# Scores, routing and dot products from an input that is not divided by its rms; head 0's query by columns as they come; w_ada tiles and gather slots reordered

## What is computed

```python
x = x + gate1 * (y_mix @ w_out)
h2 = rms_norm(x, norm2_w) * (1.0 + scale2) + shift2      # scale2, shift2 from silu(c) @ w_ada + b_ada
q = (h2 @ peer_wq)                                       # 8 heads, 2 halves of 128
s = q . peer_subkeys                                     # 2 x 128 scores a head
vals, idx = top_k(s, 16); combo = sum of pairs           # 16 x 16
top_s, pos = top_k(combo, 16); expert = ids[pos]
g = softmax(top_s); a = gelu(peer_u[expert] . h2)
x = x + gate2 * sum((g * a) * peer_v[expert])
```

## Time and profile before

| | |
|---|---|
| median of 3 runs | 1179.93 us (1179.10 to 1180.93) |
| the profiled execution, its own time | 1180.36 us |
| its span (first to last instruction) | 1178.4 us |
| PE / PEld / DVE / ACT / POOL busy | 89% / 83% / 71% / 37% / 23% |
| gathers (queue 0) | 268.45 MB, 55.0% of 16 engines' span |
| weight loads (queue 1) | 120.10 MB, 27.8% |

### The profile page before, as it was taken

How to read it: one execution, slowest core, us unless ns; L and a number is a source line. 1 busy time by engine, 2 the same in 40 slices (tenths; PEclk the granted TensorE clock), 3 DMA queues, 4 the chain that set the end, 5 groups by cost and what they waited for, 6 DMA issues and landing times.

```text
span 1178.4 us, 18884 instructions
## 1 busy us (share of the span) xinstructions
PE 1051.1 (89%) x7587; PEld 980.2 (83%) x7587; DVE 837.5 (71%) x1801; ACT 433.0 (37%) x913; POOL 268.8 (23%) x289
## 2 busy tenths in 40 slices
PE   8999987999999987777877778878999999999997
PEld 6999986998899877777877777778899888898886
DVE  7978889667667667666776766655756868765776
ACT  3635832123212221222122122211557654476452
POOL 1000005343334333333333333434000000300000
PEclk9999999999999999998999999989999999999999
DMA  9965988999999999999999999999854655455540
GB/s 371 406 244 180 348 313 307 420 421 420 421 420 420 421 420 421 420 421 420 420 420 421 420 421 422 420 422 420 325 208 161 237 205 184 147 211 179 186 171 36
DMA packets 59480, 390.35 MB, mean 331 GB/s; under 512 B 6785, under 2 KB 7809, under 8 KB 15618
## 3 DMA queue, kind: packets, MB, share of 16 engines
q0 software_dynamic: 36864, 268.45, 55.0%
q1 hardware_dynamic: 21056, 120.10, 27.8%
q10 hardware_dynamic: 1474, 0.60, 0.2%
HBM read 388.08 MB, written 1.05 MB: 330 GB/s over the span
## 4 chain that ended last, share of the span: by engine, by line
PE 63%; DMA 24%; DVE 6%; ACT 4%; issue 1%; SPq 0%; another core or an unknown queue 0%; DVEq 0%; ACTq 0%
DMA rows<-in_peer_uv,work 23%; PE aux L1566 23%; PE pj L1609 6%; PE pj L1611 5%; PE pj L1610 5%; PE aux L1545 5%; PE pj L1286 5%; PE pj L1287 4%; PE pj L1288 4%; DVE rows L2061 2%; DMA rows<-in_w_ada 1%; PE aux L1360 1%; ACT work L1142 1%; ACT rows L1010 1%; PE aux L1425 1%
## 5 line engine op out<-in xcount | busy, mean ns | idle before, releaser
L1566 PE MATMUL aux<-work,rows 128*128 128x128 f32 x2080 | 263.4, 291 | 73.8 <-ACT work L1142 73.8
L1566 PEld LDWEIGHTS aux<-work,rows 128*128 128x128 f32 x2080 | 256.2, 206 | 81.6 <-ACT work L1142 81.4
L1566 PE MATMUL aux<-work,low_pairs 128*128 128x128 f32 x2016 | 238.2, 279 | 30.2 <-ACT work L1142 30.1
L1566 PEld LDWEIGHTS aux<-work,low_pairs 128*128 128x128 f32 x2016 | 233.0, 195 | 34.0 <-ACT work L1142 34.0
L898 POOL DMA_INDIRECT rows<-in_peer_uv,work x130 | 125.5, 965 | 301.2 <-PE aux L1566 232.1
L707 DVE TENSOR_TENSOR wlo<-wring,whi 128x1024 fp32r<-128x1024 f32 x100 | 121.0, 1235 | 77.6 <-ACT whi L701 77.1
L898 POOL DMA_INDIRECT low_pairs<-in_peer_uv,work x126 | 118.3, 939 | 158.5 <-PE aux L1566 153.4
L1286 PE MATMUL pj<-xh,whi 128*128 128x256 f32 x512 | 146.3, 286 | 0.4
L1137 ACT ACTIVATE work<-work 128x4 f32<-128x4 f32 (+2 forms) x71 | 14.7, 207 | 358.3 <-DVE work L2061 358.3
L1287 PE MATMUL pj<-xl,whi 128*128 128x256 f32 x512 | 144.8, 283 | 0.0
L1288 PE MATMUL pj<-xh,wlo 128*128 128x256 f32 x512 | 144.8, 283 | 0.0
(11 more groups left out here) (288 smaller groups left out, 1461.5 us busy)
## 6 DMA issues: line engine op xcount, KB each, us to landing
wring<-in_w SPq DMA_DIRECT2D x76, 1024.0 KB, 4.8
rows<-in_w_ada SPq DMA_DIRECT2D x40, 512.0 KB, 10.1
low_pairs<-in_w_ada SPq DMA_DIRECT2D x1, 4096.0 KB, 13.4
rows<-in_w SPq DMA_DIRECT2D x3, 1024.0 KB, 10.4
rows<-in_peer_uv,work POOLq DMA_INDIRECT x130
work<-in_late_rows SPq DMA_DIRECT2D x2, 1024.0 KB, 7.5
xT<-in_gate_rows SPq DMA_DIRECT2D x2, 1024.0 KB, 7.2
rows<-in_norm_rows SPq DMA_DIRECT2D x2, 1024.0 KB, 7.3
```

What stands on the lines that cost most here:

```text
L1566: ins = mm(peer_sum[t][:, c * P:(c + 1) * P], pair(n)[:, D + c * P:D + (c + 1) * P], diag[:, n % PICKS, :], start=(n % (EXPERT_HEADS * PIC ...
```

## The change

1. **Undivided input.** `hT` becomes x * gain + r * shift, that is h2 * r. The queries, scores and dot products are then r times their values; r is positive, so the picks stay. The factor 1 / r (`token_inv`) enters as the `scale` of the softmax's exponential and of the gelu; PE turns the root to token-major (`turn_rms`), VectorE inverts two columns of it in `route(0)`.
2. **Who makes it.** ScalarE multiplies by the gain (`times_gain`, between the squares) and makes r * shift (`shift_rows`, over `work`); POOL adds the two for tile 0 (one 128x1024 addition ahead of the gathers), VectorE for tile 1 (behind `route(0)`).
3. **Head 0's query.** PE multiplies x * gain for columns 0 to 5, then 6 and 7, as they come (`early_products`, 16 products); the shift's part is a product of the weights with the shift vector alone (16 products with one column, behind `sum_v` of tile 1 and ahead of `turn_y`), and VectorE joins them: r * that + the product.
4. **Head 1** of tile 0 is also scored early (`early_query_of_head_1`), and `score_query` / `score_keys` of head 1 do tile 1 only.
5. **w_ada.** 46 tiles through the ring, two behind the projection (1 MB in place of 4 MB, slot 8). The added six are loaded behind units 12 to 14; five dot products lie between the splits of pieces 11 and 12. The shift's and gain's columns are ready before the projection.
6. **Slots.** In all rounds but the last, pick n % 12 goes to slot `FIRST_ORDER[n % 12]`; a pick waits for the last pick that had its slot.
7. `keep_busy` makes 8 fillers where it made 4; gate exponentials of groups 0 and 1 move in ScalarE's order.

```diff
-OWN_GROUPS = ((OWN_UNIT, ), (HELD_QUERY, *SUB_UNITS), FIRST_HEADS)
+OWN_GROUPS = ((OWN_UNIT, ), (HELD_QUERY, *SUB_UNITS), FIRST_HEADS[:1], FIRST_HEADS[1:])
-ADA_AFTER = {4: range(16, 21), 7: (21, 22), 8: (23, 24), 9: (25, ), 13: range(26, 29), 18: range(29, 34), 22: (34, ), 20: (35, ), 25: (36, 37), 27: (38, 39)}
+ADA_AFTER = {4: range(16, 21), 7: (21, 22), 8: (23, 24), 9: (25, ), 12: range(26, 31), 13: range(31, 34), 14: (34, 35), 18: range(36, 41), 22: (41, ), 20: (42, ),
+             25: (43, 44), 27: (45, )}
-LOWS_AMONG_PICKS = (6, 7, 7, 8, 8, 9, 10, 11)
+LOWS_AMONG_PICKS = (6, 7, 7, 8, 9, 10, 10, 11)
+FIRST_ORDER = (0, 1, 6, 7, 9, 10, 11, 2, 3, 4, 8, 5)
+LAST_ROUND = LAST_PICK // SLOTS * SLOTS - SLOTS
+def slot(n):
+    return n % SLOTS if n >= LAST_ROUND else FIRST_ORDER[n % SLOTS]
+def pick_ahead_in_slot(n):
+    return max(m for m in range(n - 2 * SLOTS, n) if m >= 0 and slot(m) == slot(n))
...
+            pool.wait_ge(gained, KC)
+            pool.wait_ge(shifted, KC)
+            pool.tensor_tensor(hT[:, :, 0:P], hT[:, :, 0:P], shift_rows[0], ALU.add).then_inc(h_ready, 1)
...
-                    if n >= SLOTS:
-                        pool.wait_ge(pair_used, n - SLOTS + 1)
+                    if n >= SLOTS:
+                        pool.wait_ge(pair_used, pick_ahead_in_slot(n) + 1)
+                    elif k in FIRST_QUERY_SLOTS:
+                        pool.wait_ge(queries, 2 * FIRST_QUERY_SLOTS.index(k) + 2)
+                    elif k == KEYS_SLOT:
+                        pool.wait_ge(expert_scores, 2)
+                    elif k in (LAST_ADA_SLOT, CONDITION_SLOT):
+                        pool.wait_ge(last_ada_used, LAST_TILES)
...
+            def times_gain(t, c):
+                nc.scalar.activation(hT[:, c, halves_[t]], xT[:, c, halves_[t]], ACT.Copy, scale=gain[:, c:c + 1]).then_inc(gained, 1)
+            def shift(t, lo, hi):
+                for c in range(lo, hi):
+                    nc.scalar.activation(shift_rows[t][:, c, :], rstd[:, halves_[t]], ACT.Copy, scale=mod[:, 3 * KC + c:3 * KC + c + 1]).then_inc(shifted, 1)
...
+            x_root(0)
+            act.wait_ge(std_ready, 2)
+            shift(0, 0, 4)
             act.wait_ge(early_scores, 1)
             nc.scalar.copy(s_all[:, 0, :], aux[:, 0, 0:2 * KEYS]).then_inc(early_scores_out, 1)
+            shift(0, 4, KC)
+            x_root(1)
...
+            for s in range(2):
+                for k in range(KC):
+                    ins = mm(aux[:, 0, s:s + 1], w_slot(first_query)[:, k, s * P:(s + 1) * P], mod[:, 3 * KC + k:3 * KC + k + 1],
+                             start=(k == 0), stop=(k == KC - 1))
+            ins.then_inc(shift_queries, 1)
             turn_y(att1, ytok, tiles=(0, ))
...
-            out_sums(4, 5)
-            out_sums(6, 7)
+            out_sums(4, 5, tiles=(0, ))
+            early_products(*range(6))
+            out_sums(6, 7, tiles=(0, ))
+            early_products(6, 7)
+            out_sums(*range(4, KC), tiles=(1, ))
...
-            keep_busy(4, 1)
-            early_scores_of_head_0()
+            early_scores_of(0)
+            turn_rms()
+            keep_busy(8, 3)
             pe.wait_ge(taken_dve, KC)
+            pe.wait_ge(h_ready, KC + 1)
             turn_h2(0)
+            early_query_of_head_1()
+            early_scores_of(1)
+            pe.wait_ge(h_scaled, KC + 1)
             score_query(0)
...
-            second_norm()
+            dve.wait_ge(std_ready, 2)
+            dve.wait_ge(shift_queries_out, 1)
+            for s in range(2):
+                dve.wait_ge(early_query, s + 1)
+                v.scalar_tensor_tensor(pq[:, 0, s, 0:P], rstd[:, 0:P], shift_query[:, s:s + 1], aux[:, 4 + s, 0:P], ALU.mult, ALU.add) \
+                    .then_inc(early_query_out, 1)
...
             route(0)
+            second_norm()
             last_ada_tiles()
```

More of the change, by code:

```diff
@@ L409, in build @@
         diag = w3.take(PICKS * P).rearrange("p (j q) -> p j q", q=P)
+        shift_rows = [work[:, t * D:(t + 1) * D].rearrange("p (c q) -> p c q", q=P) for t in range(NT)]
         s_left = w3.take(2 * KEYS).rearrange("p (s k) -> p s k", s=2)
@@ L1512, in _, with out_sums @@
                 ins.then_inc(proj, 1)
-            def out_sums(*columns):
+            def out_sums(*columns, tiles=range(NT)):
                 for k in columns:
-                    for t in range(NT):
+                    for t in tiles:
                         pe.wait_ge(squares, k + 1 if k < KC - 1 else KC + t)
@@ L1525, in _, with early_products, turn_rms @@
             whole(mixed_in, 2)
-            out_sums(4, 5)
-            out_sums(6, 7)
+            def early_products(*columns):
+                for k in columns:
+                    pe.wait_ge(gained, k + 1)
+                    for s in range(2):
+                        ins = mm(aux[:, 4 + s, 0:P], w_slot(first_query)[:, k, s * P:(s + 1) * P], hT[:, k, 0:P], start=(k == 0), stop=(k == KC - 1))
+                        if k == KC - 1:
+                            ins.then_inc(early_query, 1)
+            out_sums(4, 5, tiles=(0, ))
[3 more added lines that the diff above has]
+            out_sums(*range(4, KC), tiles=(1, ))
+            def turn_rms():
+                pe.wait_ge(std_ready, 1 + NT)
+                for t in range(NT):
+                    ins = nc.tensor.transpose(aux[:, 2, (1 + t) * P:(2 + t) * P], rstd[:, tile_of(t)], ident[:, :])
+                ins.then_inc(sums, 1)
             def turn_h2(t):
@@ L1555, in score_keys @@
                     pe.wait_ge(scores_out, h - 1)
-                for t in range(1 if h == 0 else 0, NT):
+                if h < EARLY_HEADS:
+                    pe.wait_ge(early_scores_out, h + 1)
+                for t in range(1 if h < EARLY_HEADS else 0, NT):
                     for s in range(2):
@@ L1778, in second_gain @@
                 chain.link(v.tensor_scalar(gain[:, :], part(4), 1.0, None, ALU.add))
-                chain.link(v.tensor_tensor(gain[:, :], gain[:, :], cols[:, N2W:N2W + KC], ALU.mult))
+                v.tensor_tensor(gain[:, :], gain[:, :], cols[:, N2W:N2W + KC], ALU.mult).then_inc(mod_ready, 1)
             def second_norm():
-                for t in range(NT):
-                    ts = slice(t * P, (t + 1) * P)
-                    dve.wait_ge(std_ready, 2 + t)
-                    chain.link(v.reciprocal(rstd[:, ts], rstd[:, ts]))
-                    for c in range(KC):
-                        v.scalar_tensor_tensor(hT[:, c, ts], xT[:, c, ts], gain[:, c:c + 1], rstd[:, ts], ALU.mult, ALU.mult).then_inc(h_scaled, 1)
+                dve.wait_ge(gained, NT * KC)
+                dve.wait_ge(shifted, NT * KC)
+                v.tensor_tensor(hT[:, :, P:], hT[:, :, P:], shift_rows[1], ALU.add).then_inc(h_scaled, 1)
             for z, x_in in zip((slice(0, HC), slice(HC, KC)), x_loaded):
```

153 lines of the change are left out of this document (84 added, 69 removed).

## The result

The changed kernel took 1181.68 us (median of 20 runs, 1178.93 to 1184.66), the kernel before 1179.45 (20 runs, 1177.13 to 1182.44) on the same chip: ratio 1.0018, 95% interval 1.0010 to 1.0025. It is slower by 2.2 us, where 2.2 us of gain were forecast.

The account below looks back on a forecast made before the run. The DMA gather stream, full at 421 GB/s from about 180 to 830 us, was taken as the bound. A first gather 1.0 us earlier plus 1.3 at its head gave -2.3, rounded to -2.2: median 1177.7 us, range 1175.2 to 1182.0.

Parts of the forecast that it names:

- Step 1: PE before the projection's end: 16 added one-column products take 3.7 us, less waits, so it ends 2.7 us later.
- the columns are cheap: Rival: the one-column products vanish in PE's 0.68 us wait, returning 2.7 us, time 1175.0; chance 14%.
- weights' cover: Head 0's weights land at 132.0, 0.9 us before PE is free for the one-column products; cost 0.
- Step 7: Last round of gathers: picks 242 to 245 wait for later slots, but any hole closes; cost 0, bounds 0 and 4.
- Step 4: Inside route(0): added inverse with its wait costs 0.2 us, POOL's addition slowing VectorE 0.4; bounds for the latter 0 and 2.7.
- Step 2: Moved w_ada tiles: their dot products fit into existing waits before the projection's end; cost 0.
- Step 3: From the projection's end to head 0's scores: 11.7 us becomes 7.4, saving 4.3, give or take 0.5.
- Step 5: Head of the gather stream: seven picks go to free slots, so POOL waits less; gain 1.3 us, between 0 and 2.
- Step 6: First refill of the slots: cover of 4 us before pick 20 falls to 1.7, no starving; cost 0.
- late refill: Rival: pick 12 goes out 8 us later, the stream stands still 6.3 us, net +4.1, time 1184; chance 18%.

Follow-up runs that it names:

- e3_no_columns: The changed kernel without the 16 one-column products, two columns of the shift standing in for their result; ratio 0.9975 to the kernel before.
- e9_before_columns: The kernel before with 16 one-column products in a row, result unused, added where the change has them; ratio 1.0046 to the kernel before.
- e1_gradual: The changed kernel with the slots' order going over to the plain one by swaps of neighbours from round 8; ratio 1.0003 to the kernel before.
- e2_wide: The changed kernel with each one-column product's column repeated 128 times as moving operand, one result column used; ratio 0.9987 to the kernel before.
- e7_gradual_wide: The changed kernel with both the column repeated 128 times and the slots' order changed over by swaps; ratio 0.9972 to the kernel before.
- the best version: The changed kernel with columns repeated 128 times, slot order changed by swaps, and POOL's tile 0 addition cut in two; ratios 0.9964 and 0.9958 to the kernel before.

## Why the prediction was wrong

**Step 1 failed, the products before the projection's end.** I took 3.7 us for them, less 1.0 of waits, from the row of two-column products at the full clock, and asked only how dear one instruction is. The row's price held: 3.73 and 3.69 us in the two profiles in which the clock fell late. What failed is that the price was the whole cost. In every profile of the row of narrow products the granted clock fell in it or right behind it, and the rest of the row and the 256-column products behind it pay: 5.1 us (e3_no_columns) to 5.4 us (e9_before_columns) instead of 2.7. The cost of a thing was to be read also in what runs behind it. The bound of 3.7 is below both values, though within their error. The Trainium skill, TensorE: Matmul & The Clock Gate (Part 1), states that the gate sets the clock by how busy PE has been recently, and it warns of idle gaps. In this case the clock fell without a long one: in the three profiles of the early fall PE had waited 0.22 to 0.28 us ahead of the row, and it was busy throughout when the clock fell. The rival "the columns are cheap" was further off still. The weights' cover of 0.9 us was used up: PE came to the products at 131.9 to 132.3 instead of 132.9, and in the four profiles with one-column products in the changed kernel's place it waited 0.16 to 0.28 us for them.

**Step 7 failed, the last round.** I took 0 and gave 4 as the bound; it costs 1.8 us in the times, twice (changed against e1_gradual, e2_wide against e7_gradual_wide), and 3.0 us in the profiles (gather to dot 658.1 on average of the seven with the plain last round behind the new order, 655.1 of the five with swaps). I set the issue of pick 245 against the end of 244's data, as if the DMA engines were one. They are not in step. Each gather's semaphore is raised 16 times as its data land; in the trace of the changed kernel the first and the last of the 16 lie 0.5 us apart at pick 0, 6.0 at pick 128 and 9.85 at picks 240 and 241, where all sixteen together take 2.49 us a gather. Behind the hole, at pick 242, it is 2.5. So the engines ahead run dry first, and the first delayed pick decides: 242. In the kernel before, counted at 128 packets a gather, its packets began at 794.6; now it was to be issued at the time of pick 247, 797.57, and its packets began at 798.8 in the profile after. Picks 243 to 245 then don't follow at once but as PE lets go of 236 to 239, up to 808.42.

**Step 4 was too low.** Pair sum 1.03 us dearer instead of 0.4, the inverse and its wait 0.2 as forecast; route(0) took 9.58 instead of 8.29 us, so 1.3 instead of 0.6. The bound held. The Trainium skill, GPSIMD Engine Reference (Specifications), names as those in contention the VectorE instructions with two SBUF inputs or in a 2-port mode. The trace agrees: beside the same addition the searches and replacements (FIND_INDEX8, MATCH_REPLACE8), which read one tensor, took their usual 0.28 us, and with the addition out of its way the pair sum, which reads two, lost its extra 1.02.

**Step 2 was too high.** The moved tiles cost nothing, but I had read only the tiles and not the list of low parts beside them. It removes 1.0 us of PE's waiting and a fall of the clock in some executions: by estimate 1 us, in the gain's favour.

**Step 3 was right in kind, its size low:** 11.49 to 6.20 saves 5.3 instead of 4.3, mostly since the products behind the projection ran at 112 ns each (24 from 166.72 to 169.40) and not at the 132 of the row that I scaled. **Step 5 was right, as far as the error lets it be told:** 1.6 us against 1.3. **Step 6 was right:** pick 12 at 209.90, pick 20 at 233.91, 419 GB/s from 210 to 240. The late refill did not come.

The terms by the runs: +5.1 (columns), -1.0 (list), -5.3 (step 3), +1.3 (step 4), -1.65 (step 5), +1.8 (step 7). They come to +0.2 us, where +2.2 (1.2 to 2.9) was measured. Steps 3 and 4 are from the traces, the others from times, each of these sure to about 1.5 us. The profiles say +1.4 instead of +0.15 for the last two terms together (658.1 against 656.7 on average of the four profiles with plain order throughout), and with that about 0.7 us is left, which is not assigned. So the experiments show which terms were wrong and which way, but the sum does not close better than to 1 or 2 us.

None of the rivals was what happened. The range of 1175.2 to 1182.0 held the time of 1181.68 by luck: its upper end was set for the late refill, which did not come.

## What to carry to other kernels

A row of narrow products in the middle of dense ones can cost more than its own length: 5 us for 3.7 here. Look at the granted clock of the microseconds behind it, and try the same row widened with a repeated column that nobody reads, which took 3.7 us off the time here. When a ring of buffers changes its order, price the first transfer of the switch and not the last, and change over by swaps of neighbours, which left no dip here. Before a change is priced, each list in its diff has to be laid against the waits of the engine that it feeds.

## What the runs showed of the hardware

- TensorE fell to half its clock while it was busy all the time, with float32 products of one column (32 instructions): in five profiles of five, within the row of products or right behind it, for 3.5 us (two profiles) or 10 us (three). With 128 columns: in none of six. One by one between products of 256 columns: in none of two. It also fell in or behind PE's wait of 1.0 us that ends at about 69.5 us, in three of the four profiles that have this wait, and once behind a wait of 0.78 us at 133 us (e3_no_columns).
- The 16 DMA engines drift apart in a stream of gathers 650 us long: in the changed kernel the 16 landing marks of one 1 MB gather lie within 0.5 us at its start and within 9.85 us at pick 240 (9.0 in e1_gradual), at 2.49 us a gather on average. When pick 242 was issued 13 us later than in the kernel before, the rate fell to 271 and 167 GB/s.
- A float32 instruction of one column and one of 128 columns took nearly the same time at the full clock, 3.69 to 3.84 us for 32, about 115 to 120 ns each.
- VectorE's 128x256 addition of two SBUF tensors took 1.45 us beside POOL's addition of 128x1024, ending 0.3 us behind it, and 0.43 alone.
- Executions of one kernel differ by 5 us and more (1178.9 to 1184.7 for the changed one); the best version's ten lie within 1173.9 to 1176.1. That the clock's falls and the last round make up the difference is not shown.
